# Gated linear scan: gate projection tile n + 1 in latent step n, tile 0 in the context steps, SiLU inside the last step

## The reference

```
def step(S, xs):                      # GLA, one chunk; S starts from the context's final state
    o_inter = (q_c * exp(g_c)) @ S
    attn = sum_d q_c k_c exp(g_c - g_s)            # lower triangle
    o = o_inter + attn @ v_c
    S = S * exp(g_last) + (k_c * exp(g_last - g_c)).T @ v_c
y_a = rms_norm(o_a, gdn_norm) * silu(z)            # z, gate: columns of h_lat @ w_in
y_b = rms_norm(o_b, gla_norm) * silu(gate)
y   = concatenate([y_a, y_b]) @ w_out              # latent tokens only
```

## Time and profile before

| | |
|---|---|
| median of 3 runs | 1949.39 us (1949.31 to 1950.34) |
| profiled execution, its own time | 1951.18 us |
| its span | 1949.6 us |
| granted TensorE clock, mean | 0.951 |
| block 4 | about 755.5 to 1029.3 us of the span |
| TensorE, VectorE, ScalarE, GpSimd busy over the span | 89%, 59%, 28%, 22% |

### The profile page before, as it was taken

One profiled execution on the slowest core, in us unless ns is written; L12 is line 12 of the kernel. 1 busy time (PEld: TensorE's weight loads), 2 busy tenths in 40 slices (PEclk: granted clock), 3 DMA queues, 4 the chain that ended last, 5 costly groups with the idle time before them and its releaser, 6 DMA issues. The chain is left out here.

```text
span 1949.6 us, 21922 instructions
## 1 busy us (share of the span) xinstructions
PE 1731.9 (89%) x8217; PEld 1213.4 (62%) x8217; DVE 1157.7 (59%) x1687; ACT 549.0 (28%) x879; POOL 436.1 (22%) x433
## 2 busy tenths in 40 slices
PE   3979999689876996888885995999999999999998
PEld 0134555259635995555553442888888888788786
DVE  2033555525665664667663444789898989933534
ACT  2032433256201432222222223222222222322422
POOL 3000000023201332545440112232333233400000
PEclk9989999799987997999997997999999999999999
DMA  8818110225535984000004112111111111242242
GB/s 311 307 32 338 33 32 11 73 64 165 131 89 157 266 235 134 11 22 11 22 1 161 55 63 65 44 54 44 55 44 54 44 54 45 109 150 97 87 141 86
DMA packets 200625, 189.90 MB, mean 97 GB/s; under 512 B 40405, under 2 KB 155423, under 8 KB 199260
## 3 DMA queue, kind: packets, MB, share of 16 engines
q1 hardware_dynamic: 197772, 179.01, 29.6%
q10 hardware_dynamic: 1328, 5.24, 0.7%
q0 software_dynamic: 1440, 4.46, 0.6%
HBM read 148.68 MB, written 40.01 MB: 97 GB/s over the span
## 5 line engine op out<-in xcount | busy, mean ns | idle before, releaser
L2098 PE MATMUL PS<-h2hi,whi 128*128 128x512 f32 x704 | 276.2, 392 | 18.0 <-DVE h2lo L2239 18.0
L2099 PE MATMUL PS<-h2lo,whi 128*128 128x512 f32 x704 | 275.3, 391 | 0.0
L2100 PE MATMUL PS<-h2hi,wlo 128*128 128x512 f32 x704 | 275.1, 391 | 0.0
L2252 DVE SCALAR_TENSOR_TENSOR acc<-PS,fcol,acc 128x945 f32<-128x945 f32 (+2 forms) x176 | 215.2, 1222 | 33.3 <-ACT acc L2160 27.9
L2252 DVE SCALAR_TENSOR_TENSOR act<-PS,fcol,act 128x945 f32<-128x945 f32 (+2 forms) x176 | 215.2, 1223 | 24.2 <-ACT act L2160 18.8
L429 PE MATMUL PS<-hT,wq 128*128 128x512 f32 (+1 forms) x512 | 197.2, 545 | 6.6 <-DMA wq<-in_w_in_dram 6.6
L429 PEld LDWEIGHTS PS<-hT,wq 128*128 128x128 f32 x512 | 98.0, 192 | 104.0 <-issue 94.1
L2098 PEld LDWEIGHTS PS<-h2hi,whi 128*128 128x128 f32 x704 | 133.1, 189 | 47.6 <-issue 13.5
L2214 POOL TENSOR_TENSOR wlo<-wu,whi 128x1024 fp32r<-128x1024 f32 x44 | 107.2, 2437 | 244.8 <-ACT whi L2153 244.7
L2099 PEld LDWEIGHTS PS<-h2lo,whi 128*128 128x128 f32 x704 | 133.2, 189 | 27.6
L2100 PEld LDWEIGHTS PS<-h2hi,wlo 128*128 128x128 f32 x704 | 133.1, 189 | 27.7
(11 more groups left out here) (262 smaller groups left out, 2654.5 us busy)
## 6 DMA issues: line engine op xcount, KB each, us to landing
wm<-in_w_mod_dram SPq DMA_DIRECT2D x12, 2048.0 KB, 7.9
wu<-in_w_up_dram SPq DMA_DIRECT2D x44, 512.0 KB, 3.8
wr<-in_w_down_dram SPq DMA_DIRECT2D x44, 512.0 KB, 3.5
wq<-in_w_in_dram SPq DMA_DIRECT2D x12, 512.0 KB, 3.8
gdn_x_image<-ztile SPq DMA_DIRECT2D x5, 1032.0 KB, 18.3
gdn_xt_image<-ztile SPq DMA_DIRECT2D x5, 1032.0 KB, 24.7
GR<-gdn_gc_rows SPq DMA_DIRECT2D x20, 256.0 KB, 4.4
gdn_w_image<-Wm SPq DMA_DIRECT2D x20, 256.0 KB, 3.7
```

The costliest lines, as they stand in the source:

```text
L2098: pe.matmul(PS[:, b + half, :], whi[k][u][:, kk, :], h2hi[kk][:, cols], start=(kk == 0), stop=False)
L2099: pe.matmul(PS[:, b + half, :], whi[k][u][:, kk, :], h2lo[:, kk, cols], start=False, stop=False)
L2100: mm = pe.matmul(PS[:, b + half, :], wlo[k][u][:, kk, :], h2hi[kk][:, cols], start=False, stop=(kk == KT - 1))
L2252: tp = v.scalar_tensor_tensor(out=t_[:, r0:r1, c0:c1], in0=up[:, r0 + dr:r1 + dr, c0 + dc:c1 + dc], scalar=tap_col(j, k, f), in1=t_[:, r0: ...
```

## The change

On TensorE latent step i does tile i + 1 in the places of `GATE_AT`, and the last step does none. Each of the two context steps does one half of tile 0, all 8 of its matmuls ahead of the step's transposes. ScalarE's copies follow: of tile 0 at the end of each context step, of tile i + 1 in latent step i. In the last step it applies SiLU to tiles 0 to 3 after the exponent of level 6 and to tiles 4 to 7 after Kdt, in the place of the last copy. What is computed, the loads, VectorE and GpSimd are the same.

```diff
--- before.py
+++ after.py
@@ -1533,8 +1533,10 @@
                     if lat:
                         for l in range(LEVELS):
                             level(i, l)
-                            if GATE_AT[l]:
-                                gate_part(i, *GATE_AT[l])
+                            if GATE_AT[l] and i + 1 < 2 * H:
+                                gate_part(i + 1, *GATE_AT[l])
+                    else:
+                        gate_part(0, i, 0, KT)
                     if t:
                         pe.wait_ge(s_kd2[1], t)
                     for d in range(2):
@@ -1593,8 +1595,10 @@
                             a.wait_ge(s_lk, i * LEVELS + (l + 1))
                             e = Ex[l % 2][:, :, :, :]
                             a.activation(e, e, ACT.Exp, scale=1.0 / 16).then_inc(s_lx, 1)
-                            if l == 4:
-                                gate_copy(i, 0)
+                            if l == 4 and i + 1 < 2 * H:
+                                gate_copy(i + 1, 0)
+                            if l == 6 and i + 1 == 2 * H:
+                                silus(0, 4)
                         if l == 1:
                             for d in range(2):
                                 q_factor(d, i, t, lat)
@@ -1605,12 +1609,18 @@
                     for d in range(2):
                         a.wait_ge(s_t2[d], t + 1)
                         a.activation(Kdt[d][:, :, :].rearrange("p a n -> p (a n)"), PS[:, 2, 2 * d * P:2 * (d + 1) * P], ACT.Copy).then_inc(s_kd2[d], 1)
-                    if lat:
-                        gate_copy(i, 1)
+                    if not lat:
+                        gate_copy(0, i)
+                    elif i + 1 < 2 * H:
+                        gate_copy(i + 1, 1)
+                    else:
+                        silus(4, 8)
+
+                def silus(n0, n1):
+                    a.wait_ge(s_c4, 4 * H)
+                    for n in range(n0, n1):
+                        a.activation(sz[:, n, :], sz[:, n, :], ACT.Silu).then_inc(s_sz, 1)
                 unrolled(body)
-                a.wait_ge(s_c4, 4 * H)
-                for n in range(2 * H):
-                    a.activation(sz[:, n, :], sz[:, n, :], ACT.Silu).then_inc(s_sz, 1)
 
             def halves(ap, m):
                 return ap.rearrange("p t (b h x) -> p t b h x", h=2, x=m)
```

## The result

| | before | after |
|---|---|---|
| median | 1949.39 us (5 runs, 1947.29 to 1950.54) | 1957.86 us (5 runs, 1955.93 to 1962.28) |
| profiled execution, its own time and span | 1951.18, 1949.6 us | 1957.74, 1956.1 us |
| granted clock, mean | 0.951 | 0.952 |

The change costs time: ratio 1.0046, 95% interval 1.0032 to 1.0061, or +8.5 us between the medians. Forecast were 1956.6 us and +7.2.

The account below looks back on a forecast made before the run. TensorE and VectorE take turns in latent steps; a chain with hardly any TensorE part sets the context steps. +14.9 - 0.5 - 7.2 = +7.2 us on the 1949.4 us median gives 1956.6 us; forecast 1953.3 to 1960.5, range 1951.5 to 1961.0.

Parts of the forecast that it names:

- Part 1: Context steps: tile 0's gate matmuls ahead of the transposes delay latent step 0; costs 14.9 us (12.8 to 19.7).
- The 4 us to the clock's rise: Context half 0: dense matmuls from half clock take about 4 us to raise it, so half 0 takes 9.0 us.
- Part 2: Latent steps 0 to 6 do tile i + 1: same instructions and places, another index; cost 0.
- Part 3: Clock at the starts of the latent steps, slow in steps 0 to 2 before: -0.5 us, bounds -4.3 to +3.
- Fewer slow starts than in the earlier trace: Sign of a wrong prediction: more or fewer slow latent step starts than in the profile before.
- Part 4: Last latent step without gate matmuls, its SiLU tail hidden: gives 7.2 us, after clock loss.
- The 9.2 us without clock loss: Last latent step: what the removed gate matmuls and SiLU tail would give if the clock held, 9.2 us.
- the walk: Last latent step followed by VectorE: waits and gate records go, transposes come at 1011.7, not 1018.50, together 6.8 us.
- The held clock: Rival: clock stays up in steps 0 to 2 and step 7; -0.4 us, 1949.0 us; chance 0.15 in whole or most.
- The last step that gains only its tail: Rival: last latent step gains only the 2.4 us SiLU tail; +12.0 us, 1961.4 us; chance 0.05.
- Half clock through both context halves: Rival: context halves take 13.8 us each; +11.7 us on the forecast, 1968.3 us; chance 0.03.
- The overtaking transposes: Rival: reordered queue starts context transposes first; part 1 falls to each half's 6.9 us less what hides; 2% at most.

Follow-up runs that it names:

- e1: Changed kernel with 16 unused gate matmuls (repeating tile 7) put back into the last latent step; ratio to before 1.0074.
- e4: Changed kernel with all eight SiLUs behind Kdt of the last step, as late as before the change; ratio to before 1.0041.
- e9: Changed kernel with eight unused matmuls as fillers, three behind latent step 6 and five between levels of the last step; ratio to before 1.0034.
- e6: Changed kernel without tile 0's gates: context steps hold one small identity matmul and do not wait for hT; 1944.04 us, ratio to before 0.9962.
- e2: Changed kernel with one gate matmul instead of eight in each context step, all waits kept; ratio to before 0.9999.
- e7: e3 with ScalarE's copies of tile 0 moved later too, behind context step 1's decay factors and latent step 0's second exponent; ratio to before 1.0009.
- e3: Changed kernel with each context step's eight gate matmuls behind its state product instead of ahead of its transposes; ratio to before 1.0039.
- e8: Kernel before with SiLUs moved earlier and the last step's unread transposes, Kdt, state product and Sbd update left out; ratio to before 0.9967.
- e10: Kernel before with three idle matmuls at the end of each of latent steps 0 to 6; ratio to before 0.9989.
- e11: e8 with three idle matmuls behind each of latent steps 0 to 6; 1940.29 us, ratio to before 0.9952.
- e12: e7 without last state work, with idle matmuls behind steps 0 to 6 and in the last step; 1940.00 us, ratio to before 0.9956.

## Why the prediction was right, and where it was off

**Part 1** (14.9 predicted, 16.0 measured). The chain was as told: hT, half 0, transposes, Kdt, state product, half 1, transposes, Sbd, Qbd. Seven records ran at half clock and not five, so half 0 took 9.9 and not 9.0 us. The 4 us to the clock's rise came from a misread row: the stretch just ahead of the earlier trace rows shows that the clock was up until 777 and had only then fallen, so it was not a start from the lower level.

```profile
774.00:777.00 3.00, 0.35 (x2) 1.00 0.88 278
```

After the change TensorE worked 6.1 us before the clock rose. How long half 0 runs slow also changes by run: in e1, e4 and e9, with the same context steps, the first Qbd comes at 35.2, 35.8 and 36.7 us, which makes part 1 15.0 to 16.5. Half 1 found its load landed, as told. The first Qbd itself took 1.34 us instead of 0.85, beside GpSimd's work for step 0, which before the change had ended 0.2 us ahead of it; that adds 0.5 behind the mark. e6 shows that nearly all of the price lies here.

**Part 2** (0 predicted). Steps 1 to 6 after the change take 30.6 to 30.7 us, as steps 3 to 6 did before, with no wait for weights.

**Part 3** (-0.5, bounds -4.3 to +3). This pair of profiles has 220.45 against 216.65 for the seven steps, so -3.8: after the change only step 0 started slowly, 32.73 us. Fewer slow starts than in the earlier trace rows was one of the prediction's own signs of being wrong, though it had called their number chance. It is: e1, e2, e4, e6 and e7 run the same seven steps in 222.0 to 222.4 us, e9 in 219.3 and e3 in 216.7. So the sum of the three marks, +4.4, is the chance of this pairing. Profiles of like clock give more: after against e8, both without slow steps 1 and 2 and alike up to the last step, 16.0 + 0.5 - 7.8, or +8.7; with the slow steps in both, 222.0 against 220.5, about +9.8. The +8.5 of the medians lies near these. Adding the sum to the median and not to the profiled time was the better choice: the profiled run of before was 1.8 us above its median, that of after 0.1 below.

**Part 4** (7.2 predicted, 7.8 measured). The 9.2 us without clock loss are what e9 shows, 33.08 against 23.85, and its transposes come 6.8 us earlier, as the walk had it. Of the 2.0 us taken off for half clock 1.4 came, but at another place. The prediction let half clock cost nothing in the middle of the step and 2.0 in the tail. In the trace the transposes came only 5.4 us earlier and not 6.8, so the middle lost 1.4, and from there to the last add it took 8.37 us against 8.38: the clock was up again by the transposes and the tail lost nothing. The number is near because one error stood in for the other. Kdt was hidden and SiLU ended ahead of the last add, as told. Four other profiles (e2, e4, e6, e7), with the transposes at 16.5 us, lie between.

**Rivals.** The held clock would have given 1949.0; it would need all slow starts gone, and the fillers show what that takes. The last step that gains only its tail is refuted by e1; at 1961.4 us it would have lain just outside the stated range, which the prediction says takes it in. Half clock through both context halves did not come: it rose after 6.1 us. The overtaking transposes did not come either. The drain that the Trainium skill, ScalarE: Activation LUTs, section What ACT_TABLE_LOAD costs, adds to a table switch was not seen here; 1.29 to 1.30 us from the load's start to the first SiLU's was all, in before, after and e4.

The error of the forecast, 1.3 us, can't be divided. By the marks part 1 was 1.1 too low, part 4 0.6 too low as a gain, and part 3 3.3 too high, which would make +4.4, not +8.5; the rest is which step starts each execution draws and what the other blocks take. That the sum came so near is in part luck.

## What to carry to other kernels

A step that is moved to where an engine looks idle takes its waits along: ask, on each in-order queue that it enters, what is queued behind it, and when its inputs land. e3 moved the matmuls out of the way and won little until ScalarE's copies moved too. Short idle holes of TensorE ahead of dense work can cost more than the work that would fill them, so an unused matmul in a hole can be worth its while.

## What the runs showed of the hardware

The same steps, in the same code, took 30.7 us each or 33.4 and 32.1 for steps 1 and 2, by the clock at their start, and with three idle matmuls in the hole (3.5 to 0.9 us) none of three profiles (e10, e11, e12) shows slow steps from step 1 on; of eleven without them there three are spared (after, e3, e8), so a single profile proves little. In the changed kernel's last step the clock fell a second time, behind a stretch with 2.1 us of matmuls in 5.0, and rose again before its tail. SP issued the second half of hT, behind the landing of the first, 10.5 to 12.1 us after the block's start over the profiles; the price of part 1 starts to count there.
